# Weights moved in quarter blocks through a stream of four, with more blocks kept on the chip, and an opening that puts the first tile's chain first

## The reference

```python
q = (xc @ w_query).reshape(T, 8, 2, 128)
s = einsum('thpd,hpnd->thpn', q, sub_keys)        # 128 scores a half
s_top, i_top = top_k(s, 16)                        # 16 best of each half
cand = s_top[:, :, 0, :, None] + s_top[:, :, 1, None, :]   # 256 sums
g_s, sel = top_k(cand, 16); g = softmax(g_s)       # 16 experts a head
idx = i_top[..., 0] * 128 + i_top[..., 1]          # of the selected
a = einsum('td,thkd->thk', xc, expert_u[idx])      # a gathered row each
y = einsum('thk,thkd->td', g * gelu(a), expert_v[idx])
```

## Time and profile before

| | |
|---|---|
| median of three runs | 2398.11 us |
| the profiled execution's own time | 2397.24 us |
| its span, first to last instruction | 2395.4 us |
| mean granted TensorE clock | 0.873 of full speed |
| bytes moved by the DMA engines | 961.71 MB, mean 401 GB/s |
| gathers | 768, first issued at 128.69 us, last at 2369.7 us |

### The profile page before, as it was taken

One profiled execution on the slowest core, in us unless ns is written; L12 is line 12 of the kernel. 1 busy time (PEld: TensorE's weight loads), 2 busy tenths in 40 slices (PEclk: granted clock), 3 DMA queues, 4 the chain that ended last, 5 costly groups with the idle time before them and its releaser, 6 DMA issues.

```text
span 2395.4 us, 20005 instructions
## 1 busy us (share of the span) xinstructions
PE 1759.3 (73%) x5782; PEld 910.7 (38%) x5782; DVE 1731.4 (72%) x3603; ACT 898.5 (38%) x2596; POOL 940.8 (39%) x772
## 2 busy tenths in 40 slices
PE   7878877787797426887506768887877778787776
PEld 3543435435463115463103333542333354322222
DVE  3378887787678887688898687688768758864444
ACT  2234753352234332233313362334256424443333
POOL 0034554244334454333455344333434524443332
PEclk9899788888899858898858878989977899999999
DMA  5299999999999999999999999999999999999997
GB/s 233 108 383 421 415 422 422 422 402 421 422 420 416 421 393 423 422 418 422 421 422 417 421 408 417 422 406 422 399 423 404 421 422 420 412 421 422 422 421 310
DMA packets 127408, 961.71 MB, mean 401 GB/s; under 512 B 14913, under 2 KB 15041, under 8 KB 20289
## 3 DMA queue, kind: packets, MB, share of 16 engines
q0 software_dynamic: 110592, 805.36, 81.3%
q1 hardware_dynamic: 16704, 155.07, 15.6%
HBM read 959.32 MB, written 1.05 MB: 401 GB/s over the span
## 4 chain that ended last, share of the span: by engine, by line
DMA 50%; PE 19%; DVE 16%; issue 7%; ACT 6%; POOL 2%; DVEq 0%; SPq 0%; ACTq 0%; POOLq 0%
DMA ring<-in_uv,idx 49%; PE y L1111 10%; DVE ring L1484 6%; DVE x L1475 6%; PE acc L954 3%; PE acc L965 3%; POOL ring L912 2%; ACT diag L1282 1%; ACT wgt L1272 1%; PE y L954 1%; ACT L1269 1%; ACT ge L1269 1%; PE tp L1040 1%; DMA wbuf<-in_wts 1%; PE sc L1061 0%
## 5 line engine op out<-in xcount | busy, mean ns | idle before, releaser
L912 POOL DMA_INDIRECT ring<-in_uv,idx x768 | 940.6, 1225 | 1429.7 <-PE y L1111 878.4
L1111 PE MATMUL y<-ring,diag 128*128 128x512 f32 x2020 | 1070.9, 672 | 502.5 <-ACT diag L1282 489.1
L1484 DVE CUSTOM_DVE_ANT_0 ring<-ring,h 128x1024 f32<-128x1024 f32 x768 | 933.2, 1221 | 479.9 <-DMA ring<-in_uv,idx 478.5
L1111 PEld LDWEIGHTS y<-ring,diag 128*128 128x128 f32 x2020 | 394.3, 209 | 1120.8 <-ACT diag L1282 735.0
L1269 ACT ACTIVATE ge<-a 128x1 f32<-128x1 f32 x768 | 155.2, 202 | 1237.7 <-DVE a L1484 1235.3
L1475 DVE SCALAR_TENSOR_TENSOR x<-ring,wgt,x 128x1024 f32<-128x1024 f32 x263 | 337.2, 1282 | 61.1 <-ACT wgt L1272 50.4
L965 PE MATMUL acc<-fT,wbuf 128*128 128x128 f32 x2048 | 247.2, 283 | 23.6 <-issue 17.9
L965 PEld LDWEIGHTS acc<-fT,wbuf 128*128 128x128 f32 x2048 | 245.5, 200 | 38.7 <-issue 38.7
L954 PE MATMUL acc<-wbuf,fT 128*128 128x512 f32 (+2 forms) x472 | 216.9, 614 | 28.8 <-DMA wbuf<-in_wts 23.3
L1272 ACT ACTIVATE wgt<-ge,gate 128x1 f32<-128x1 f32 x768 | 226.2, 295 | 25.1
L1282 ACT ACTIVATE diag<-id_s,wgt 128x128 f32<-128x128 f32 x505 | 202.7, 401 | 16.5
(11 more groups left out here) (148 smaller groups left out, 1025.8 us busy)
## 6 DMA issues: line engine op xcount, KB each, us to landing
wbuf<-in_wts SPq DMA_DIRECT2D x58, 2048.0 KB, 12.1
ring<-in_uv,idx POOLq DMA_INDIRECT x768, 12.8
caches<-in_wts SPq DMA_DIRECT2D x3, 2048.0 KB, 9.7
kept<-in_wts SPq DMA_DIRECT2D x3, 2048.0 KB, 17.0
kbuf<-in_keys SPq DMA_DIRECT2D x24, 256.0 KB, 8.5
gain<-in_gains SPq DMA_DIRECT2D x11, 512.0 KB, 12.2
wbuf<-in_wts SPq DMA_DIRECT2D x2, 1664.0 KB, 10.7
wbuf<-in_wts SPq DMA_DIRECT2D x2, 1280.0 KB, 10.3
```

The lines of the kernel that those rows point to most:

```text
L912: nc.gpsimd.indirect_dma_start(ring[:, n % RING, :], None, uv[layer(s)], bass.IndirectOffsetOnAxis(ap=idx[:, tile(s), k:k + 1], axis=0),). ...
L1111: mm = nc.tensor.matmul(y[half][:], diag[:, (d - 1) % DIAGS, :], ring[:, n % RING, D + half * BLK:D + (half + 1) * BLK], start=(k == y_end ...
L1484: ins = v.tensor_tensor_reduce(u, u, h[:, tile(s), :], 1.0, 0.0, ALU.mult, ALU.add, a[:, c:c + 1])
```

## The change

- **Quarters.** A weight block is loaded as four DMAs of 4 KB a partition, two k-tiles each. `wbuf` becomes a stream of four quarters (16 KB a partition instead of 32), and a product waits for one quarter at a time. All products are cut in four parts on PE, so rows can stand between them.
- **Kept blocks.** The freed room holds `wkeep` (two blocks) beside the one in `caches`. Eleven blocks are now loaded once for both tiles, two of them (qkv0, qkv1) in ring slots 0 to 3 before the first gather needs those. Besides, q2 and q3 of layer 1 are loaded once and used for both tiles (`SHARED`): step 2's top-k of blocks 2 and 3 then comes after step 3's mixer and norm. A second `fT` holds both tiles' transposed inputs.
- **Ring.** It has 8 slots instead of 7, and 5 diagonals instead of 6.
- **Gains.** They are loaded once as 56 rows of 128 floats (28 KB). PE spreads a row over the partitions by products with a column of the identity (`gain_rows`), and DVE reads it from PSUM.
- **Opening.** The second tile's qkv work is a list of its own (`ahead`). The planner takes from it only where the first tile's work would wait by more than half the item's length.
- **First top-k.** Block 0 of step 0 is done head by head (`0a`, `0b`), so 16 rows can be gathered after half the work.

```diff
-RING = 7
-DIAGS = 6
+RING = 8
+DIAGS = 5
+QUARTER = WBLK // 4
+STREAM = 4
...
+def queries(s):
+    late = SHARED[layer(s)]
+    both = [(b, (s - 1, s)) for b in late] if tile(s) else []
+    return both + [(b, (s,)) for b in range(4) if b not in late]
...
-OPENED = ("qkv1", "qkv2")
-KEPT = [[(0, "qkv0"), (0, "out0"), (1, "c0")], [(0, "out1"), (1, "u0"), (2, "q")]]
+SHARED = [(), (2, 3), ()]
+KEPT = [[(0, "out0"), (1, "c0")],
+        [(0, "out1"), (1, "u0"), (2, "q")],
+        [(0, "qkv2"), (0, "q0"), (1, "c1"), (2, "k")],
+        [(0, "qkv0")],
+        [(0, "qkv1")]]
...
+        if ahead_of[engine]:
+            item = ahead_of[engine][0]
+            at, main = ready(item), ready(dense_of[engine][0])
+            if at is not None and (main is None or main > max(at, free[engine]) + 0.5 * item[2]):
+                yield at, 4, item
...
+                elif what in ("w", "kept"):
+                    first, size = quarters(name)[j]
+                    src = wts[W_BASE[layer(s)] + number, :, first:first + size]
+                    last = before_load(what, s, name, j)
+                    if last:
+                        sp.wait_ge(acc_done.sem, acc_done.count(last[0], last[1:]))
+                    ...
+                        n = STREAMED.index((s, name, j))
+                        sp.dma_start(wbuf[:, n % STREAM, 0:size], src).then_inc(w_in[n % STREAM], 16)
...
+            def gain_rows(s, which):
+                for half in range(2):
+                    for c in range(4):
+                        one = id_s[0:n, 8 * row + 4 * half + c:8 * row + 4 * half + c + 1].broadcast_to([n, P])
+                        mm = nc.tensor.matmul(gain_bank(s, which, half)[:, c * P:(c + 1) * P], one, gain[0:n, :],
+                                              start=True, stop=True)
+                mm.then_inc(gain_done.sem, 1)
```

More of the change, by code:

```diff
@@ L168, in normed, with products, product @@
     def normed(which, x_ready):
[L169 removed]
+        gain = put("PE", "gain", which, US["gain"])
+        h = put("DVE", "norm", which, US["norm"], gain, put("ACT", "rms", which, US["rms"], x_ready, table="sqrt"))
         turns = [put("PE", "turn", f"{which}{i}", US["turn"], h) for i in range(2)]
         return [put("ACT", "copy", f"{which}{i}", US["take"], turns[i]) for i in range(2)][1]
[L173 to L177, removed]
+    def products(uses, *before, us=None):
+        for j in range(parts_of(uses[0][1])):
+            for step, name in uses:
+                cost = us or US["quarter_T" if transposed(s, name) else "quarter"]
+                put("PE", "mm", name, cost, *before, part=j, step=step)
+        return [(step, "mm", name, parts_of(name) - 1) for step, name in uses]
+    def product(name, *before, us=None):
+        return products([(s, name)], *before, us=us)[0]
     def taken(name, *before, table=None, **kw):
@@ L253, in dense @@
     last = normed("ffn", x)
[L254 to L268, removed]
@@ new lines, in dense @@
+    todo = queries(s)
+    for i, (b, steps) in enumerate(todo):
+        if s == 0 and i > 0:
+            picked(*todo[i - 1])
+        made = products([(step, f"q{b}") for step in steps], *[(step, "copy", "ffn1", 0) for step in steps])
+        for step, mm in zip(steps, made):
+            put("ACT", "take", f"q{b}", US["take"], mm, step=step)
+        if i > 0:
+            if s > 0:
+                picked(*todo[i - 1])
+            best(*todo[i - 1])
+    picked(*todo[-1])
+    best(*todo[-1])
@@ L275, in opening, with block_of, quarters @@
 def opening():
[L277 to L301, removed]
-OPENED = ("qkv1", "qkv2")
-KEPT = [[(0, "qkv0"), (0, "out0"), (1, "c0")], [(0, "out1"), (1, "u0"), (2, "q")]]
+    ahead = [(kind, "mix") for kind in ("gain", "rms", "norm")]
+    ahead += [(kind, f"mix{i}") for kind in ("turn", "copy") for i in range(2)]
+    ahead += [(kind, f"qkv{i}") for kind in ("mm", "take") for i in range(3)]
+    ahead += [(kind, f"qk{i}") for kind in ("sq", "root", "rope") for i in range(3)]
+    second = dense(1)
+    return (dense(0) + [x for x in second if x[1][1:3] not in ahead], [x for x in second if x[1][1:3] in ahead])
+SHARED = [(), (2, 3), ()]
[4 more added lines that the diff above has]
+        [(0, "qkv1")]]
+def block_of(name):
+    return {"uq0": "ups", "uq1": "ups", "uk": "ups", "uv": "ups", "bra0": "bra", "bra1": "bra",
+            "brb0": "brb", "brb1": "brb"}.get(name, name)
+def quarters(name):
+    if name == "ups":
+        return [(0, 768), (768, 768), (1536, 1024)]
+    size = 832 if name == "lat" else QUARTER
+    return [(j * size, size) for j in range(4)]
 def kept_place(l, name):
@@ L391, in schedule @@
     done = {("x", 0): 7.0, ("x", 1): 20.0}
-    work = opening() + [x for s in range(2, STEPS) for x in dense(s)]
+    work, ahead = opening()
+    work += [x for s in range(2, STEPS) for x in dense(s)]
     dense_of = {e: [x for x in work if x[0] == e] for e in ("PE", "ACT", "DVE")}
+    ahead_of = {e: [x for x in ahead if x[0] == e] for e in ("PE", "ACT", "DVE")}
     order = {e: [] for e in ("PE", "ACT", "DVE")}
```

641 lines of the change are left out of this document (344 added, 297 removed).

## The result

The kernel after takes 2384.38 us, the median of five runs (2380.57 to 2389.46); the kernel before, run beside it, 2397.39 (2396.66 to 2398.49). The ratio is 0.9945, with a 95% interval of 0.9934 to 0.9957: 13 us faster, where the forecast was 38 us (2360). The gain was forecast three times too large: the prediction was wrong. That the time lies inside the range of 2344 to 2388 is luck, since the upper end stood there for a rival (step 2's index late) that cost little in this kernel.

What follows compares the result with a forecast made beforehand. The prediction took the kernel to be bound by bytes on the DMA wire after the first gather: -16.9 us (earlier first gather), -25.6 (fewer bytes), +5 (idle wire), sum -37.5, so 2360 us, range 2344 to 2388.

Steps and rivals of the forecast that it cites:

- step 2's index late: Rival: row 64 of step 2 needs step 3's mixer, streamed blocks come late, wire idles; 2387 us, chance 0.13.
- What bounds the kernel: Whole kernel: bytes on the wire after 128.7 us, tile 0's dense chain on PE and DVE before.
- The first gather: Opening: earlier start, filled PE gaps and split top-k bring it from 128.7 to about 112 us, -16.9 us.
- Bytes behind the first gather: After the first gather: fewer weights, gains and keys, priced with 4 KB rows, save 25.6 us, between 12 and 38.
- The price of 4 KB rows: Weight loads after the first gather: 2.477 us a MB instead of 2.379, about 4% more.
- The failed step: Wire beside gathers: slower weight loads only slow dense work, the wire stays full; +5 us over today's loss.
- The slack argument: Dense work beside gathers: it can bear slower loads, as PE waited for `wbuf` only 23.3 us in all.
- Dense work late in every step: Rival: steps 2 to 5 stream 46 blocks, each 7.5 us late; at 25% turned to idle wire 2441 us, chance 0.09.
- Ring better: Rival: the eighth ring slot also closes today's dips in the wire; 2340 us, chance 0.09.
- Opening PE-bound: Rival: a denser PE drops longer to its lower clock, only the least savings come; 2374 us, chance 0.10.
- Fixed part on the wire: Rival: 182 more loads each pay their fixed part as wire time, +670 us; 3030 us, chance 0.01.

Runs made afterwards that it cites:

- e8: The kernel before without nine of its loads of gains, so the output is not the reference's: 2387.20 us.
- e11: e6 with no shared query blocks (q2, q3 of layer 1 and their keys loaded in both steps): 2356.61 us.
- e12: e6 with step 0's first top-k in one piece of two heads instead of head by head: 2353.86 us.
- e1: The kernel before with each weight block loaded as four DMAs of 4 KB rows, same order and buffers: 2446.71 us.
- e2: The change with one planner edit: loads queue behind each other, each taking at most three times its own wire time: 2373.28 us.
- e4: The change with loads in half blocks of 8 KB rows, two halves of stream in the same room, products still in four parts: 2360.99 us.
- e3: The change with a ring of 7 slots instead of 8 and a stream of 6 quarters instead of 4: 2376.14 us.
- e10: The change with 8 KB rows, 7 ring slots and a stream of three half blocks (e6 without the planner's edit): 2347.04 us.
- e5: e4 with the planner letting loads follow each other, each at most twice as long as alone: 2371.96 us.
- e9: e6 with quarter loads of 4 KB rows, its planner allowing a load three times its own time instead of twice: 2357.85 us.
- e6: e5 with 7 ring slots instead of 8 and a stream of three half blocks instead of two: 2348.62 us.
- e7: The kernel before with each weight block loaded as two DMAs of 8 KB rows, awaited together: 2401.98 us.

## Why the prediction was wrong, step by step

- **What bounds the kernel: right.** From the first gather on it is the wire. e8, e11 and e12 each moved the end by about what their bytes or their start say.
- **The first gather: right in kind, small in size.** -21.0 us for -16.9; q0's start gave 13.9 of it, where I took 10.5, and the rest 7.1. e12 has the split top-k at 5.3 where I took 6.4. Part of the surplus was not foreseen: up to q0 PE ran at a granted clock of 1.00 instead of 0.90. The range was too narrow as well: the bounds of its three terms sum to -3 and -21.6, not to -5 and -21.
- **Bytes behind the first gather: too many taken off.** I took 16.0 MB, and it was 12.8 (131.86 to 119.08). "About equally many bytes of weights lie ahead of the first gather" was false: they wait behind an earlier start. And nine loads of gains went, not ten. Together 3.2 MB, 7.9 us.
- **The price of 4 KB rows: too low.** I read 2.477 from one lone load. Over the stretch it is 300.5 us for 119.08 MB, 2.523, which is 5.5 us more; the gathers' own packets took 2.424 us a MB for 2.418, another 5 us, for which I have no cause.
- **The failed step: "by it the gathers simply gain what the weights lose ... The wire stays full, only the dense work is slower", +5 us.** I had priced a block beside gathers at 14.8 us and seen PE's demand, but not joined the two: one block of stream and a landing of 13 us give the weights some 140 GB/s beside gathers, and the buffer of before held twice the bytes. The dense work came late against an order that did not know it, and in place of a full wire the idle wire rose from 13.5 to 26.9 us, +13.4. e1 shows this with the old order and the old buffer (21 us of idle wire from the rows alone), and e2 shows that the order matters (both dips close). The remedies took back 23 us (rows, e4), 8 (depth, e3), 11 (the planner, e2), and 37 (rows and depth, e10). Each of these also rewrote the order, so how the 13.4 us divide among row, depth and order stays open. The slack argument failed too: "before, PE waited for `wbuf` 23.3 us in all" (28.9 with the waits of L965) is no measure of how late a load may be in a written order.
- The four misses sum to 7.9 + 5.5 + 5.2 + 8.4 = 27 us. The stretch from the first gather to the last `X` was forecast at 2237.5 us and took 2262.1, 24.6 more; shares rounded to a tenth leave 2 us open. The opening gave 4.1 back.
- **Rivals.** *Dense work late in every step* had the mechanism, but not the place: it came mostly in the two steps of layer 2 (slice 12, beside layer 1's dense work, lost some too), with 13 us of idle wire for the 86 priced. *Step 2's index late*: in the change POOL waited for that gate 11.4 us, covered by the gathers in flight. Where the order put it later it did appear (behind 320 dot products: 31.9 us in e2, 30.5 in e4, with slices of 305 and 335 GB/s), and in e2 and e5 the same befell step 5's first index. *Ring better*: its trade is the reverse; a slot given for half a block of stream won 8 us (e3) and 14 (e10). What the eighth slot is worth by itself no run tells. *Opening PE-bound*: refuted, since with a denser PE the granted clock was 1.00, not under 0.90, and the first gather went out at 107.7 us. *Fixed part on the wire*: refuted by e9, 124 more loads of weights than e6 for 9 us, which the price of the rows covers. (The 2.0 us that the prediction gives from the Trainium skill stand in "DMA: Bandwidth & Descriptors" under "Anatomy of one DMA", for DMAs issued from GpSimd; these loads are issued from SP, and the forecast did not use them.)

## What to carry to other kernels

A load's row length sets both its price and its share of the wire beside other traffic, so when loads are cut finer to wait less, keep the rows at 8 KB; cutting them along the other axis may do it too, but no run here tried that. For each stream of buffers, work out bytes in flight over landing and use, under the traffic that will be beside it, and compare that with what the consumer takes in its densest stretch; a mean over the kernel hides it. Under a fixed order lateness is not paid in proportion (e7 lost no idle wire, e1 21 us), so test the reserve and the order too, not only the speed. When an edit makes a planner write a new order, look at where the first index of each step lands: most of the wire left idle in e2, and most of the 11 us of e5, was lost there.

## What was not expected of the hardware

The price of a weight's byte rose with every halving of the row, more than a lone load showed: 2.38 us a MB at 16 KB, 2.42 to 2.43 at 8 KB (e4, e7, e10), and 2.50 to 2.55 at 4 KB (e9, the change, e1). Within the 4 KB rows it was least where PE waited least for the loads (e9). A load of a quarter of the bytes landed no sooner than a whole block had: 12.9 us against 12.1. And the denser opening had the higher clock: from 35 us to q0 the granted clock was 0.87 to 0.91 in the kernel before and in e1, e7 and e8, and 1.00 in the change and in each of the nine kernels made from it, with PE busy for 96% to 97% of the stretch instead of 82% to 84%. Whether the density is the cause no run shows.
